# One projection for query, key and value of an attention unit, scored two steps after it

## The chip, the cores and the metric

The kernel runs on one core of one Trainium2 chip. The metric is the device time of one execution in microseconds (us). The core has five engines that run side by side, each through its own instructions in the order in which they are written: TensorE (PE in the profile; its weight loads are PEld), VectorE (DVE), ScalarE (ACT), GpSimd (POOL) and SyncE (SP, which here only starts DMA transfers). They wait for one another through semaphores.

## The reference

A trunk of two layers on 1024 tokens of width 1024: dilated attention, MLP, mLSTM, MLP, all with residuals. The change is in the attention, of which this is what is computed:

```
qkv = (x @ w_in).reshape(b, s, 3, 3 groups, 16 heads, 64)
for g, (window, dilation) in enumerate(((128, 1), (512, 4), (2048, 16))):
    q = rms_norm(qkv[:, :, 0, g], q_gain[g]) * 64 ** -0.5
    k = rms_norm(qkv[:, :, 1, g], k_gain[g])
    # causal; a query at t sees t, t-d, ..., t-window (129 keys at most)
    o, l = dilated_window_attention(q, k, qkv[:, :, 2, g], rel_bias[:, g], window, dilation)
wts = softmax over the three groups of the log-denominators l
y = sum over groups of wts * o;  x = x + y @ w_out
```

## The kernel before

The attention phase goes through 24 **sections**, one for each pair of heads (8) and group (3): section 3p+g is pair p, group g. A section has eight **tiles** of 128 tokens and eight **units** of 128 queries. All matmuls are "split": each f32 operand is held as a high part (`_hi`) and a rest (`_lo`), and `split_matmul` (L67) issues three matmuls, hi·hi (L69), lo·hi (L70), hi·lo (L71).

The work is written as **supersteps** `st` of eight **steps** `j` (`run_supersteps`; 4 supersteps in line, a loop of 3 rounds of 6, the rest in line). Every engine has its own `step(i, st, j)`, and the order in it is the order on that engine. A step `T = 8·st + j` of TensorE does, one after another:

- query and key of tile T (`ps_qk`): 8 row blocks k, three matmuls each with 256 columns; the stationary operand is the tile of the normed input, `hT_hi[:, k, j*P:(j+1)*P]`;
- three transposes into `ps_t`: normalised query and key of tile T-1 (`qkn`) and value (`vT`) of a tile of the section before; once in a while the row statistics `stat`;
- the transposes of the probabilities `prob` of unit U-1 into `ps_p`, where U = T-8: units are scored one superstep after their projection;
- a quarter of the value projection of half a section (`ps_v`), six matmuls of 512 columns, value transposed (`w_hi` stationary);
- the scores of unit U (`ps_s`), and probabilities times value of unit U-1 (`ps_o`, called the PV product below).

ScalarE in a step: exp of unit U-1 (`prob`, L635), copies of `ps_o` (L651, L652), the high part of a weight block (`w_hi`, L602), then `sq`, the squares of `ps_qk` of tile T (L667), which wait until that projection is done, then `pT_hi` (L673, the high part of the transposed probabilities), `qk_hi` (L684) and `v_hi` (L688). VectorE: bias and maximum of the unit's scores (L723, L726), `ss` and `var` (L732, L737) out of `sq`, `pT_lo` (L743), `qk_lo` (L758), `v_lo` (L764), `qkn` (L779), and in some steps the merge of the three groups of a pair (`merge_step`, L794 to L847). GpSimd: `w_lo` and the inverse root `rs`. SyncE loads the weight blocks 12 steps ahead.

Units of group 0 but for the first, and every second unit of group 1, also have the 128 keys before them (`has_prev`): their scores are 256 columns wide and their PV product has six matmuls instead of three. There are 88 of these **wide** units and 104 **narrow** ones. The tokens of groups 1 and 2 are reordered (stride 4, stride 16) when ScalarE and VectorE write `qk_hi`, `qk_lo` and `vT` (`perm_view`, `perm_dest`).

Of the kernel before, what the change touches and what calls it, by code (L numbers as in the profile page):

```python
# [29 lines left out]
NG = len(GROUPS)  # L30
HEADS = 16
# [17 lines left out]
def bias_onehot():  # L49

    out = np.zeros((NG, REL_BUCKETS + 1, BIAS_LEN), np.float32)
    exact = REL_BUCKETS // 2
    for g, (window, dilation) in enumerate(GROUPS):
        band = window // dilation
        for x in range(BIAS_LEN):
            step = x - (P - 1)
            if step < 0 or step > band:
# [16 lines left out]
def perm_view(ap, g, width):  # L74

    if g == 0:
        return ap
    return ap.rearrange("p (i r) -> p r i", r=GROUPS[g][1])


def perm_dest(buf, g, t0, width):

    if g == 0:
        return buf[:, t0:t0 + width]
    d = GROUPS[g][1]
    if g == 1:
        n, i0 = t0 // HALF, (t0 % HALF) // d
        return buf.rearrange("p (r n i) -> p r n i", r=d, n=2)[:, :, n, i0:i0 + width // d]  # L90
    return buf.rearrange("p (r i) -> p r i", r=d)[:, :, t0 // d:(t0 + width) // d]


def natural_view(buf, g):
# [5 lines left out]
    return buf.rearrange("p (r i) -> p i r", r=16)  # L100


def split_tokens(ap, g):
# [5 lines left out]
    return ap.rearrange("p (i r) -> p i r", r=16)  # L109


# [192 lines left out]
LAST_SUPER = SECTIONS + 2  # L304
# [18 lines left out]
class AttentionBuffers:  # L323


    def __init__(self, nc, ctx):
        sb = lambda n, s: ctx.enter_context(nc.sbuf_tensor(n, s, F32))
        self.vT = sb("vT", [P, 2, SEQ])
# [4 lines left out]
        self.x_tiles = [b[:, i, :] for b in (self.vT, self.o_g0, self.w_bc) for i in range(2)]  # L333
# [3 lines left out]
def attention_phase(nc, ones, ident, buffers, total, norm_gain, hT_hi, hT_lo, wqkv, q_gain, k_gain, bias_dram, yT_dram):  # L337
# [3 lines left out]
    with ExitStack() as ctx:  # L341
# [8 lines left out]
        qk_hi = sb("qk_hi", [P, 2, 2, SEQ], F32R)  # L350
        qk_lo = sb("qk_lo", [P, 2, 2, SEQ], F32R)
        v_hi = sb("v_hi", [P, 3, P], F32R)
        v_lo = sb("v_lo", [P, 3, P], F32R)
# [13 lines left out]
        vT, w_bc, prob = buffers.vT, buffers.w_bc, buffers.prob  # L367
        o_raw = [buffers.o_g0, total[:].rearrange("p (o t) -> p o t", o=1), buffers.o_g2]
        ring = sb("ring", [P, HALF])
        compact = sb("compact", [64, NG, 2, 2, 16])  # L370
        top = sb("top", [64, 2, 16])
        diff = sb("diff", [64, NG, 2, 16])
        grown = sb("grown", [64, NG, 2, 16])
        part = sb("part", [64, NG, 2, 16])
        den = sb("den", [64, 2, 16])
        share = sb("share", [64, NG, 2, 16])

        ps_qk = [ps(f"ps_qk{i}", [P, HALF]) for i in range(2)]
        ps_v = ps("ps_v", [P, HALF])
# [12 lines left out]
        qk_mm, v_mm, turned = sem("qk_mm"), sem("v_mm"), sem("turned")  # L392
# [4 lines left out]
        vT_done = sem("vT_done")  # L397
# [12 lines left out]
        def has_unit(st, j, back):  # L410

            return TT <= TT * st + j - back < TT * (SECTIONS + 1)

        def unit(st, j, back):

            sec, u = divmod(TT * (st - 1) + j - back, TT)
            return sec, u
# [6 lines left out]
        def _(sp):  # L424
# [4 lines left out]
            sp.dma_start(gains[HD:P, 1, :], k_gain).then_inc(gains_in, 16)  # L429
            for n in range(TT + 4):  # L430
# [4 lines left out]
            def step(i, st, j):  # L435
# [5 lines left out]
                if j == 2 and st < SECTIONS:  # L441
                    g, pair = st % NG, st // NG + 2 * i
                    if st >= NG:
                        sp.wait_ge(neg_done, TT * N - 2 * TT)
                    if st == 1:
                        norm.wait_all(sp)
                    base = (g * HEADS + 2 * pair) * BIAS_LEN
                    if g < 2:
                        sp.dma_start(bias[g][:], bass.AP(bias_dram.tensor, base, [[1, P], [BIAS_LEN, 2], [1, 2 * P]]))\
                            .then_inc(bias_in[g], 16)  # L450
                    else:
                        sp.dma_start(bias[g][0:64], bass.AP(bias_dram.tensor, base, [[1, 64], [BIAS_LEN, 2], [1, P]]))\
                            .then_inc(bias_in[g], 16)
                        sp.dma_start(bias[g][64:P, :, 0:64],
                                     bass.AP(bias_dram.tensor, base + 64, [[1, 64], [BIAS_LEN, 2], [1, 64]]))\
                            .then_inc(bias_in[g], 16)
                if j == 2 and 2 <= st <= SECTIONS + 1 and (st - 2) % NG < 2:
                    g, pair = (st - 2) % NG, (st - 2) // NG + 2 * i
# [5 lines left out]
                    for s in range(2):  # L464
                        for h in range(2):
                            src = stat_dram[g, s, h]
                            if g == 0:
                                sp.dma_start(compact[:, g, s, h, :], src.rearrange("(p c) -> p c", c=16))\
                                    .then_inc(compact_in[g], 16)
                            else:  # L470
                                sp.dma_start(compact[:, g, s, h, :].rearrange("p (r c) -> p r c", r=4),
                                             src.rearrange("(r p c) -> p r c", r=4, c=4)).then_inc(compact_in[g], 16)
                if j == 5 and st >= 4 and (st - 4) % NG == 0:
                    pair = (st - 4) // NG + 2 * i
                    sp.wait_ge(share_done, pair + 1)
                    sp.dma_start(share_dram.rearrange("g h (p c) -> p (g h) c", c=16),
# [6 lines left out]
                if j == 0 and st >= 5 and (st - 5) % NG == 0:  # L483
                    pair = (st - 5) // NG + 2 * i
# [1419 lines left out]
```

## Time and profile before

| | us |
|---|---|
| median of three runs | 3387.8 (3387.46 to 3390.41) |
| the profiled execution | 3383.74 |
| its span, first to last instruction | 3382.0 |
| TensorE busy over the span | 3192.3 (94%) |
| VectorE, ScalarE, GpSimd busy | 1334.0, 1102.1, 825.2 |
| mean granted TensorE clock | 0.978 of full |

The attention phase reaches from the first `ps_qk` matmul at 34.94 us to the first matmul of the next phase at 1332.47 us. The last projection matmul of it starts at 1266.80 us; what follows until 1332.47 is the tail: the last section's units, the last merge, the store of its result and the load of it by the next phase. Starts of instructions in a timeline are exact to 0.01 us; a matmul's duration is longer than the distance to the next one, since matmuls overlap in the array, so that distances between starts are what they cost. In the same way an instruction of ScalarE or VectorE may be started before the one ahead of it has ended.

### The profile page before, as it was taken

Reading aid. Unit: us, or ns where it says so; the run is one execution under the profiler, and the core shown is the slowest. Engines: PE = TensorE matmul, PEld = TensorE weight load, DVE = VectorE, ACT = ScalarE, POOL = GpSimd, SP = SyncE. Lnnn points to the kernel's source line nnn. Section 1 sums busy time; section 2 is a strip of 40 time slices with the busy share of each in tenths; the row PEclk is TensorE's granted clock in tenths of the full one; section 3 lists DMA queues with packets and bytes.
Section 4 is the critical chain, followed back from the end, with each engine's and each line's share of the span. In section 5 each row is a group of like instructions: output and inputs, shape, how many; then the busy total and the mean of one; then the engine's idle time right before and its main releaser. Section 6 shows DMA issues by size and latency. Waiting matters only on the chain. (4 is left out here: it accounts for less than half of the span.)

```text
span 3382.0 us, 48256 instructions
## 1 busy us (share of the span) xinstructions
PE 3192.3 (94%) x17466; PEld 2669.5 (79%) x17466; DVE 1334.0 (39%) x3725; ACT 1102.1 (33%) x3002; POOL 825.2 (24%) x598
## 2 busy tenths in 40 slices
PE   4999999999999995999999999899877999999999
PEld 3888888888888883878888888678655788888887
DVE  6445454555555554341313133541064431313131
ACT  4555555555555553321111112210244211111020
POOL 3332333333233320212222122112111122222221
PEclk9999999999999995999999999999998999999999
DMA  2112121211112114111111111111201111111112
GB/s 98 36 40 59 41 58 40 61 49 50 52 45 53 47 32 150 50 44 47 48 50 44 50 50 45 38 44 50 81 26 57 44 50 44 50 50 44 50 45 80
DMA packets 89904, 177.01 MB, mean 52 GB/s; under 512 B 25515, under 2 KB 55870, under 8 KB 89662
## 3 DMA queue, kind: packets, MB, share of 16 engines
q1 hardware_dynamic: 87358, 169.63, 16.1%
q10 hardware_dynamic: 2304, 4.20, 0.3%
q8 instruction: 147, 2.41, 0.3%
q14 instruction: 95, 0.78, 0.1%
HBM read 160.67 MB, written 13.12 MB: 51 GB/s over the span
## 5 line engine op out<-in xcount | busy, mean ns | idle before, releaser
L69 PE MATMUL ps_qk<-w_hi,attn_hT_hi 128*128 128x256 f32 x1536 | 437.4, 285 | 23.3 <-DVE attn_hT_lo L213 9.7
L915 POOL TENSOR_TENSOR first_w_lo<-first_raw,first_w_hi 128x1024 fp32r<-128x1024 f32 x96 | 231.7, 2414 | 900.8 <-ACT first_w_hi L911 900.8
L70 PE MATMUL ps_qk<-w_lo,attn_hT_hi 128*128 128x256 f32 x1536 | 436.1, 284 | 0.0
L71 PE MATMUL ps_qk<-w_hi,attn_hT_lo 128*128 128x256 f32 x1536 | 436.1, 284 | 0.0
L857 POOL TENSOR_TENSOR w_lo<-raw,w_hi 128x384 fp32r<-128x384 f32 x192 | 194.6, 1015 | 701.9 <-ACT w_hi L602 701.9
L915 POOL TENSOR_TENSOR second_w_lo<-second_raw,second_w_hi 128x1024 fp32r<-128x1024 f32 x72 | 172.2, 2391 | 630.0 <-ACT second_w_hi L911 630.0
L69 PEld LDWEIGHTS ps_qk<-w_hi,attn_hT_hi 128*128 128x128 f32 x1536 | 294.1, 191 | 27.6 <-issue 13.3
L635 ACT ACTIVATE prob<-ps_s,neg_max 128x128 f32<-128x128 f32 (+1 forms) x384 | 156.6, 413 | 439.7 <-DVE neg_max L726 439.7
L70 PEld LDWEIGHTS ps_qk<-w_lo,attn_hT_hi 128*128 128x128 f32 x1536 | 294.7, 192 | 0.4
L71 PEld LDWEIGHTS ps_qk<-w_hi,attn_hT_lo 128*128 128x128 f32 x1536 | 294.9, 192 | 0.0
L69 PE MATMUL first_ps<-first_hid_hi,first_w_hi 128*128 128x512 f32 x640 | 255.4, 399 | 32.7 <-DVE first_hid_lo L1239 32.7
L732 DVE TENSOR_REDUCE ss<-sq 128x4 f32<-128x256 f32 x192 | 80.7, 420 | 506.9 <-ACT sq L667 506.9
L69 PE MATMUL first_ps<-first_hT_hi,first_w_hi 128*128 128x512 f32 x640 | 252.6, 395 | 14.2 <-POOL first_w_lo L915 14.2
L69 PE MATMUL second_ps<-second_hid_hi,second_w_hi 128*128 128x512 f32 x640 | 251.0, 392 | 12.5 <-DVE second_hid_lo L1242 12.5
L70 PE MATMUL first_ps<-first_hid_lo,first_w_hi 128*128 128x512 f32 x640 | 254.9, 398 | 0.0
L71 PE MATMUL first_ps<-first_hid_hi,first_w_lo 128*128 128x512 f32 x640 | 254.7, 398 | 0.0
L70 PE MATMUL first_ps<-first_hT_lo,first_w_hi 128*128 128x512 f32 x640 | 251.4, 393 | 0.0
L71 PE MATMUL first_ps<-first_hT_hi,first_w_lo 128*128 128x512 f32 x640 | 251.4, 393 | 0.0
L70 PE MATMUL second_ps<-second_hid_lo,second_w_hi 128*128 128x512 f32 x640 | 250.5, 391 | 0.0
L71 PE MATMUL second_ps<-second_hid_hi,second_w_lo 128*128 128x512 f32 x640 | 250.1, 391 | 0.0
L879 POOL TENSOR_TENSOR rs<-var,minus_half 128x4 f32<-128x4 f32 x192 | 193.3, 1007 | 133.5 <-DVE var L737 125.0
L911 ACT CAST first_w_hi<-first_raw 128x1024 fp32r<-128x1024 f32 x96 | 99.9, 1041 | 383.6 <-PE first_ps L71 358.5
(276 smaller groups left out, 6853.9 us busy)
## 6 DMA issues: line engine op xcount, KB each, us to landing
raw<-in_wqkv SPq DMA_DIRECT2D x192, 192.0 KB, 2.3
first_raw<-in_w SPq DMA_DIRECT2D x64, 512.0 KB, 3.4
second_raw<-in_w SPq DMA_DIRECT2D x64, 512.0 KB, 3.4
w_bc<-share_dram SPq DMA_DIRECT2D x48, 256.0 KB, 4.2
first_raw<-in_vo_pieces SPq DMA_DIRECT2D x16, 512.0 KB, 3.5
bias<-bias_dram SPq DMA_DIRECT2D x16, 256.0 KB, 3.6
yT_dram<-o_g SPq DMA_DIRECT2D x8, 512.0 KB, 3.1
first_raw<-in_attn_wo SPq DMA_DIRECT2D x8, 512.0 KB, 3.5
```

Of the source, the lines that this page charges most:

```text
L69: pe.matmul(out, a_hi, b_hi, start=first, stop=False)
L70: pe.matmul(out, a_hi, b_lo, start=False, stop=False)
L71: return pe.matmul(out, a_lo, b_hi, start=False, stop=last)
L635: a = act.activation(prob[:, u % 2, h, c0:2 * P], ps_s[h][:, c0:2 * P], ACT.Exp, bias=neg_max[:, sp_, h * TT + u:h * TT + u + 1], accum_ou ...
L732: dve.tensor_reduce(ss[:], sq[:].rearrange("p (h e) -> p h e", e=HD), AX.X, ALU.add)\
L857: pool.tensor_tensor(w_lo[:, par, k, :], raw[:, slot, :], w_hi[:, par, k, :].bitcast(F32), ALU.subtract).then_inc(w_lo_done, 1)
L879: pool.tensor_tensor(rs[:], var[:], minus_half[:], ALU.pow).then_inc(rs_done, 1)
L911: act.copy(self.hi[:, n % 2, :], self.raw[:, n % self.RAW, :]).then_inc(self.hi_done, 1)
L915: pool.tensor_tensor(self.lo[:, n % 2, :], self.raw[:, n % self.RAW, :], self.hi[:, n % 2, :].bitcast(F32), ALU.subtract).then_inc(self.lo ...
```

## The change

A section's value is projected together with its query and key: each tile has one projection of 384 columns into `ps_qkv`, 24 matmuls. The value comes out with its tokens on the partitions, so that `vT`, its copies and its transposes go; ScalarE writes `v_hi` and VectorE `v_lo` straight from `ps_qkv`. The reordering of tokens moves to the stationary operand: the tile of group 1 reads the normed input with a stride of 4 elements, that of group 2 with a stride of 8 (`tile_view`), where a unit of group 2 now mixes two residues and the bias masks the other one. With that a tile is a unit, and units are scored two steps after their projection (`LAG = 2`) instead of eight. The projection is cut in two: five of its eight row blocks, then the transposes of `qkn` and `prob`, then the last three blocks. `qk_hi`, `qk_lo` hold one section instead of two. The merge has one copy less and stands at other steps; the tail has one superstep less. In the diff `LAG` is 2 and `EARLY_TILES` is 5; the wait on `v_lo_done` stands ahead of the PV product, beside those on `pT_hi` and `pT_lo`; `turned_probabilities` writes `pT_hi`.

```
-            U = T - TT
+            U = T - LAG
@@ TensorE
-                for k in range(KT):
-                    mm = split_matmul(pe, ps_qk[j % 2][:, 0:2 * P],
-                                      hT_hi[:, k, j * P:(j + 1) * P], hT_lo[:, k, j * P:(j + 1) * P],
-                                      w_hi[:, par, k, 0:2 * P], w_lo[:, par, k, 0:2 * P], k == 0, k == KT - 1)
-                mm.then_inc(qk_mm, 1)
+            def project(k_first, k_end):
+                for k in range(k_first, k_end):
...
+                    mm = split_matmul(pe, ps_qkv[j % 2][:, 0:W3],
+                                      tile_view(hT_hi[:, k, :], st % NG, j), tile_view(hT_lo[:, k, :], st % NG, j),
+                                      w_hi[:, par, k, :], w_lo[:, par, k, :], k == 0, k == KT - 1)
+                return mm
+            if st < SECTIONS:
...
+                project(0, EARLY_TILES)
...
-                    mm = pe.transpose(ps_t[:, 2 * P:3 * P], vT[:, (st - 1) % 2, j * P:(j + 1) * P], ident[:])
...
-                for k in range(2 * (j % 4), 2 * (j % 4) + 2):
-                    mm = split_matmul(pe, ps_v[:], w_hi[:, par, k, 2 * P:3 * P], w_lo[:, par, k, 2 * P:3 * P],
-                                      hT_hi[:, k, half * HALF:(half + 1) * HALF],
-                                      hT_lo[:, k, half * HALF:(half + 1) * HALF], k == 0, k == KT - 1)
+                project(EARLY_TILES, KT).then_inc(qkv_mm, 1)
...
+                pe.wait_ge(v_lo_done, U)
@@ ScalarE
-                act.copy(perm_dest(vT[:, vp, :], g, HALF, HALF), perm_view(ps_v[:], g, HALF)).then_inc(vT_done, 1)
...
-                act.wait_ge(qk_mm, T + 1)
+                act.wait_ge(qkv_mm, T + 1)
                 if TT * st + j >= 1:
                     act.wait_ge(reduced, T)
-                act.activation(sq[:], ps_qk[j % 2][:, 0:2 * P], ACT.Square).then_inc(squared, 1)
+                act.activation(sq[:], ps_qkv[j % 2][:, 0:2 * P], ACT.Square).then_inc(squared, 1)
+                act.copy(v_hi[:, j, :], ps_qkv[j % 2][:, 2 * P:W3]).then_inc(v_hi_done, 1)
...
+            turned_probabilities()
@@ VectorE
+                dve.wait_ge(v_hi_done, T + 1)
...
+                dve.tensor_tensor(v_lo[:, j, :], ps_qkv[j % 2][:, 2 * P:W3], v_hi[:, j, :].bitcast(F32), ALU.subtract)\
+                    .then_inc(v_lo_done, 1)
@@ reordering
+def tile_view(ap, g, u):
+    if g == 0:
+        return ap[:, u * P:(u + 1) * P]
     if g == 1:
+        return ap.rearrange("p (n i r) -> p r n i", n=2, r=4)[:, u // 2, u % 2, :]
+    return ap.rearrange("p (m u) -> p u m", u=TT)[:, u, :]
```

What now stands where. First TensorE, from the end of one tile's projection on; in it `ps_qk` and `ps_qkv` are the projections, `ps_s` the scores, `ps_o` the PV product, rows that only repeat are left out. Before:

```order
L71 MATMUL ps_qk<-w_hi,attn_hT_lo 128x256
L526 MATMUL ps_t<-ident,qkn 128x128 x2
L530 MATMUL ps_t<-ident,vT 128x128
L547 MATMUL ps_p<-ident,prob 128x128 x2
L69 MATMUL ps_v<-attn_hT_hi,w_hi 128x512
...
L71 MATMUL ps_s<-qk_hi,qk_lo 128x128
L69 MATMUL ps_o<-pT_hi,v_hi 128x256
```

And now:

```order
L75 MATMUL ps_qkv<-w_hi,attn_hT_lo 128x384
L517 MATMUL ps_t<-ident,qkn 128x128 x2
L534 MATMUL ps_p<-ident,prob 128x128 x4
L73 MATMUL ps_qkv<-w_hi,attn_hT_hi 128x384
...
L75 MATMUL ps_qkv<-w_hi,attn_hT_lo 128x384
L73 MATMUL ps_s<-qk_hi 128x256
...
L75 MATMUL ps_s<-qk_hi,qk_lo 128x256
L73 MATMUL ps_o<-pT_hi,v_hi 128x256
```

Between the last matmul of a tile's projection and the PV product there stood the transposes, a quarter of the value projection and the scores; now only the scores stand there.

Then ScalarE, in the middle of a step: `sq` is the instruction that waits for the tile's projection, `pT_hi` what the PV product waits for. Before:

```order
L602 CAST w_hi<-raw 128x384
L664 REGISTER_ALU
L667 ACTIVATE sq<-ps_qk 128x256
L673 CAST pT_hi<-ps_p 128x512
L684 ACTIVATE qk_hi<-ps_t,gains 128x4x32 x2
L688 CAST v_hi<-ps_t 128x128
```

And now:

```order
L577 CAST w_hi<-raw 128x384
L630 REGISTER_ALU
L633 ACTIVATE sq<-ps_qkv 128x256
L634 CAST v_hi<-ps_qkv 128x128
L640 CAST pT_hi<-ps_p 128x512
L648 ACTIVATE qk_hi<-ps_t,gains 128x128 x2
```

`v_hi` has moved from behind `pT_hi` to ahead of it; `pT_hi` stands behind `sq` in both.

## Rows read from the trace of the kernel before

**Rows 1.** Busy time by stretch: inside the attention, and its tail.
```profile
core 0: us, PE busy (x) PEld busy (x) DVE busy (x) ACT busy (x) POOL busy (x), PEclk, DMA share, GB/s
400.00:500.00 100.00, 96.54 (x722) 85.59 (x721) 58.09 (x223) 53.23 (x185) 30.31 (x30) 1.00 0.20 56
1269.00:1333.00 64.00, 24.47 (x107) 17.10 (x108) 23.41 (x91) 19.58 (x79) 2.34 (x1) 0.52 0.26 79
```

**Rows 2.** Timeline of TensorE, one wide step: start, us, operation.
```profile
1033.96 0.38 PE L526 MATMUL ps_t<-ident,qkn 128*128 128x128 f32 x2
1034.17 0.27 PE L530 MATMUL ps_t<-ident,vT 128*128 128x128 f32 x1
1034.28 0.60 PE L547 MATMUL ps_p<-ident,prob 128*128 128x128 f32 x4
...
1034.95 0.39 PE L70 MATMUL ps_v<-attn_hT_lo,w_hi 128*128 128x512 f32 x1
...
1035.88 0.40 PE L71 MATMUL ps_v<-attn_hT_hi,w_lo 128*128 128x512 f32 x1
1036.20 0.39 PE L69 MATMUL ps_s<-qk_hi 64*128 64x256 f32 x2
...
1036.77 0.38 PE L69 MATMUL ps_o<-pT_hi,v_hi 128*128 128x256 f32 x1
...
1037.57 0.28 PE L69 MATMUL ps_qk<-w_hi,attn_hT_hi 128*128 128x256 f32 x1
...
1040.32 0.29 PE L71 MATMUL ps_qk<-w_hi,attn_hT_lo 128*128 128x256 f32 x1
1040.44 0.38 PE L526 MATMUL ps_t<-ident,qkn 128*128 128x128 f32 x2
```

**Rows 3.** Timeline of ScalarE, the same step and the next.
```profile
1034.85 0.39 ACT L667 ACTIVATE sq<-ps_qk 128x256 f32<-128x256 f32 x1
1035.13 0.58 ACT L673 CAST pT_hi<-ps_p 128x512 fp32r<-128x512 f32 x1
...
1036.11 0.28 ACT L688 CAST v_hi<-ps_t 128x128 fp32r<-128x128 f32 x1
1036.31 0.59 ACT L625 COPY vT<-ps_v 128x512 f32<-128x512 f32 x1
...
1039.44 0.20 ACT L635 ACTIVATION_READ_ACCUMULATOR prob<-ps_s,neg_max 128x1 f32 x1
...
1040.64 0.38 ACT L667 ACTIVATE sq<-ps_qk 128x256 f32<-128x256 f32 x1
```

**Rows 4.** Timeline of VectorE, the same step.
```profile
1035.26 0.42 DVE L732 TENSOR_REDUCE ss<-sq 128x4 f32<-128x256 f32 x1 [2.62 <-ACT sq L667]
1035.72 0.23 DVE L737 TENSOR_SCALAR var<-ss 128x4 f32<-128x4 f32 x1
1035.86 0.68 DVE L743 TENSOR_TENSOR pT_lo<-ps_p,pT_hi 128x512 fp32r<-128x512 f32 x1
```

**Rows 5.** Groups by form, 0 to 1400 us: narrow units.
```profile
L743 DVE TENSOR_TENSOR pT_lo<-ps_p,pT_hi 128x256 fp32r<-128x256 f32 x104 | 44.0, 423 | 16.5 <-ACT pT_hi L673 16.2
...
L673 ACT CAST pT_hi<-ps_p 128x256 fp32r<-128x256 f32 x104 | 38.9, 374 | 17.0 <-PE ps_p L547 17.0
```

**Rows 6.** Timeline of GpSimd in the first section, where no units run.
```profile
84.82 1.01 POOL L879 TENSOR_TENSOR rs<-var,minus_half 128x4 f32<-128x4 f32 x1 [2.49 <-DVE var L737]
...
89.29 1.01 POOL L879 TENSOR_TENSOR rs<-var,minus_half 128x4 f32<-128x4 f32 x1 [2.48 <-DVE var L737]
```

**Rows 7.** Timelines of TensorE and VectorE in the tail.
```profile
1266.80 0.40 PE L71 MATMUL ps_v<-attn_hT_hi,w_lo 128*128 128x512 f32 x1
...
1300.05 0.42 DVE L743 TENSOR_TENSOR pT_lo<-ps_p,pT_hi 128x256 fp32r<-128x256 f32 x1 [2.03 <-ACT pT_hi L673]
...
1300.58 0.55 PE L69 MATMUL ps_o<-pT_hi,v_hi 128*128 128x256 f32 x1 [0.97 <-DVE pT_lo L743]
```

**Rows 8.** Groups by form: merge operations, with strided and with contiguous reads.
```profile
L837 DVE TENSOR_TENSOR w_bc<-w_bc,total 128x1024 f32<-128x1024 f32 x8 | 16.0, 2003 | 0.9 <-DMA w_bc<-share_dram 0.9
...
L840 DVE TENSOR_TENSOR o_g<-o_g,w_bc 128x1024 f32<-128x1024 f32 x8 | 9.7, 1213 | 0.0
```

More of the change, by code:

```diff
@@ L54, in bias_onehot @@
         band = window // dilation
+        mixed = dilation // UNIT_STRIDE[g]
         for x in range(BIAS_LEN):
-            step = x - (P - 1)
-            if step < 0 or step > band:
+            step, other = divmod(x - (P - 1), mixed)
+            if step < 0 or step > band or other:
                 out[g, REL_BUCKETS, x] = 1.0
@@ L349, in attention_phase @@
         gains = sb("gains", [P, 2, NG])
[L350 to L353, printed above, removed]
+        qk_hi = sb("qk_hi", [P, 2, SEQ], F32R)
+        qk_lo = sb("qk_lo", [P, 2, SEQ], F32R)
+        v_hi = sb("v_hi", [P, TT, P], F32R)
+        v_lo = sb("v_lo", [P, TT, P], F32R)
         sq = sb("sq", [P, 2 * P])
@@ L366, in attention_phase @@
         stat_rows = sb("stat_rows", [4 * TT, P])
-        vT, w_bc, prob = buffers.vT, buffers.w_bc, buffers.prob
+        w_bc, prob = buffers.w_bc, buffers.prob
         o_raw = [buffers.o_g0, total[:].rearrange("p (o t) -> p o t", o=1), buffers.o_g2]
         ring = sb("ring", [P, HALF])
[L370 to L379, printed above, removed]
+        compact = sb("compact", [P, NG, 2, 2, TT])
+        top = sb("top", [P, 2, TT])
+        diff = sb("diff", [P, NG, 2, TT])
+        grown = sb("grown", [P, NG, 2, TT])
+        part = sb("part", [P, NG, 2, TT])
+        den = sb("den", [P, 2, TT])
+        share = sb("share", [P, NG, 2, TT])
+        ps_qkv = [ps(f"ps_qkv{i}", [P, HALF]) for i in range(2)]
         ps_t = ps("ps_t", [P, HALF])
@@ L429, in _, with load_bias @@
             sp.dma_start(gains[HD:P, 1, :], k_gain).then_inc(gains_in, 16)
+            def load_bias(g, pair):
+                base = (g * HEADS + 2 * pair) * BIAS_LEN
+                width = 2 * P if g < 2 else P
+                sp.dma_start(bias[g][:], bass.AP(bias_dram.tensor, base, [[1, P], [BIAS_LEN, 2], [1, width]]))\
+                    .then_inc(bias_in[g], 16)
+            load_bias(0, 0)
             for n in range(TT + 4):
@@ L440, in step @@
                     sp.dma_start(raw[:, j % 4], wqkv[T + 12]).then_inc(raw_in[j % 4], 16)
[L441 to L445, printed above, removed]
-                        norm.wait_all(sp)
[L447 to L458, printed above, removed]
+                if j == 5 and st + 1 < SECTIONS:
+                    if st + 1 >= NG:
+                        sp.wait_ge(neg_done, TT * N - TT)
+                    if st == 0:
+                        norm.wait_all(sp)
+                    load_bias((st + 1) % NG, (st + 1) // NG + 2 * i)
+                if j == 4 and 1 <= st <= SECTIONS and (st - 1) % NG < 2:
+                    g, pair = (st - 1) % NG, (st - 1) // NG + 2 * i
                     rows = 2 * pair + g + 1
@@ L768, in step @@
-                if j == 0:
-                    turned_tiles()
-                    turned_probabilities()
-                else:
-                    turned_probabilities()
-                    turned_tiles()
+                turned_probabilities()
+                if 1 <= TT * st + j <= TT * SECTIONS:
+                    dve.wait_ge(turn_hi, T)
+                    if j == 3 and st >= 1 and (st - 1) % NG < 2:
+                        if st >= 2:
+                            dve.wait_ge(rows_out, 16 * (2 * ((st - 1) // NG + 2 * i) + (st - 1) % NG))
+                        dve.tensor_copy(stat_rows[:], ps_t[0:4 * TT, 3 * P:4 * P]).then_inc(rows_done, 1)
+                    sec, t = divmod(TT * st + j - 1, TT)
+                    g = sec % NG
+                    for a in range(2):
+                        ins = dve.scalar_tensor_tensor(qk_lo[:, a, t * P:(t + 1) * P], ps_t[:, a * P:(a + 1) * P],
+                                                       gains[:, a, g:g + 1], qk_hi[:, a, t * P:(t + 1) * P].bitcast(F32),
+                                                       ALU.mult, ALU.subtract)
+                    ins.then_inc(turn_lo, 1)
```

218 lines of the change are left out of this document (76 added, 142 removed).

## The prediction, made before the changed kernel had run

> **What bounds the kernel now.** I first read busy time by stretch: inside the attention TensorE is busy 96.5 of 100 us at a granted clock of 1.00, the others 30 to 58 us [rows 1]. So TensorE sets the pace there, and a change to the attention is worth what it does to TensorE's step. The tail is different: 24.5 us busy in 64, clock 0.52 (the 1.2 GHz level) [rows 1]; there a chain through all engines sets the pace.
>
> Then I read one wide step on TensorE, start to start: it takes 40.44 - 33.96 = 6.48 us. Its 24 projection matmuls of 256 columns take 40.44 - 37.57 = 2.87 us, 0.120 each; a value matmul of 512 columns takes (35.88 - 34.95)/4 = 0.233; the transpose of vT 0.11; scores 0.57, PV 0.80 [rows 2]. The reader is to see that there is no hole: what PV needs is ready when TensorE comes to it. Last, the same step on ScalarE and VectorE [rows 3, 4], for what is ready when. It shows how far the feeding chain is from its limit: pT_lo ends at 1035.86 + 0.68 = 1036.54 and PV starts at 1036.77, 0.23 us later. That cover was the transposes, the value matmuls and the scores, which stand between a tile's projection and PV.
>
> **The change, part by part.**
>
> *TensorE's own work.* vT's transpose goes, -0.11 per step. 24 matmuls of 256 and 6 of 512 columns (24 x 0.120 + 6 x 0.233 = 4.27) become 24 of 384. No row has 384 columns; between 0.120 and 0.233 that is 0.176, sum 4.23, so -0.03 with the last digits kept. Together -0.14 us per step, if the stationary operand read with a stride costs nothing (below).
>
> *The wait that is new.* In a step of the changed program TensorE goes: five blocks, transposes (prob of unit U-1 among them), three blocks, scores, PV of unit U-1. ScalarE makes pT_hi for that PV behind sq, and sq waits for the whole projection, whose end now lies behind the transposes. So pT_hi cannot start while the last three blocks run, though its input is there, and v_hi is put ahead of it as well. Let 0 be the start of the last projection matmul. Its result is out at about 0.34 (0.29 at 256 columns, 0.40 at 512 [rows 2]). sq followed a projection's end by 0.03 (40.32 + 0.29 to 40.64 [rows 2, 3]): sq at 0.37. The next on ScalarE, v_hi, 0.28 later (34.85 to 35.13), pT_hi 0.20 behind v_hi (36.11 to 36.31) [rows 3]: pT_hi at 0.85. It takes 0.58 (wide) [rows 3] or 0.37 (narrow) [rows 5], so it ends at 1.43 or 1.22. VectorE meanwhile: ss at 0.37 + 0.39 + 0.02 = 0.78, var 0.46 and pT_lo at the earliest another 0.14 later, 1.38 [rows 4]. So pT_lo starts at 1.46 (wide, after pT_hi, with 0.03 for the hop) or 1.38 (narrow, after var); it takes 0.68 [rows 4] or 0.42 [rows 5] and ends at 2.14 or 1.80. TensorE began PV 0.11 after pT_lo's end where it had waited for it (1300.05 + 0.42 to 1300.58 [rows 7]): PV at 2.25 or 1.91. Without a wait TensorE would be there at 0.27 + 0.57 = 0.84: the last matmul 0.18 plus the 0.09 by which 35.88 to 36.20 exceeds 0.233, then the scores [rows 2]. The wait is 1.41 us in wide and 1.07 us in narrow steps.
>
> Behind the waiting PV on TensorE is the whole next projection, and for its end sq of the next step waits: nothing catches up, each step pays. There are 88 wide units and 104 narrow ones [rows 5], of which the last three run behind the last projection. 88 x (1.41 - 0.14) = 112 and 101 x (1.07 - 0.14) = 94, together **+206 us**.
>
> *The other ring: exp.* The transposes of prob wait for exp, which waits for the maxima, which stand on VectorE behind pT_lo, qk_lo and qkn. Before, exp of the next unit ended at 39.64, 4.79 us after sq's start at 34.85 [rows 3]. Now v_hi ahead of pT_hi adds 0.20 to ScalarE's part of it and the late v_lo changes nothing, so exp ends near 0.37 + 4.79 + 0.20 = 5.36. TensorE comes to those transposes at 2.25 + 0.80 (PV) + 15 x 0.176 + 0.21 (qkn) = 5.90 in a wide step. It is hidden, by 0.5 us; had PV not waited it would be the bound, at 4.49 against 5.36. The merge on VectorE (up to 2.00 us in one step [rows 8]) uses that slack up and pushes some steps. It did before too: the exp that ended at 39.64 ran 1.1 us ahead of the transposes that followed 0.33 us after 40.44 [rows 2, 3]. The slack has shrunk by half a microsecond in the seven or so merging steps of a pair, while a copy has gone: 0 to +25 us over 8 pairs. I take 0, since the merge is the same work and several of its pieces are shorter than the slack, and keep the 25 in the range.
>
> *Starting early and the tail.* Six steps of the first section now carry units. Without units a step took 89.29 - 84.82 = 4.47 us [rows 6], with a wide one 6.48: six times 2.0 less the first narrow unit's part is **+11 us**. In the tail 1300.58 - 1266.80 = 33.8 us go by from the last projection matmul to the last PV [rows 7], ten steps of 3.4 us. Now three steps are left, of which the first also ends a loaded one: 3 x 3.4 + 2.5 = 12.7, **-21 us**. The merge, store and load behind it are the same in length. SyncE's queue has the same transfers per step, one bias transfer less per pair, and the weight blocks are loaded 12 steps ahead as before, now with longer steps.
>
> *Sum.* +206 + 11 - 21 = **+196 us**. The profiled execution took 3383.7 us (span 3382.0 and 1.7 around it) and the median of the runs is 3387.8, 4.1 more; 3387.8 + 196 = **3584 us**.
>
> *What I can't read here: the strided weight load.* 128 of the 192 tiles (groups 1 and 2) load their stationary operand with a stride of 4 or 8 elements; no row shows TensorE doing that. From below: a transpose loads new weights too and takes 0.11 us (34.17 to 34.28 [rows 2]), so the load can be that long at most; VectorE's reads with a stride took 2003 / 1213 = 1.65 times as long [rows 8]; 0.11 x 1.65 = 0.18, against 0.176 for the matmul that hides it: +0.005 x 24 x 128 = 15 us. From above: if it took twice as long, 0.22, then 0.044 x 24 x 128 = +135 us, all of it on the path, since the projection lies in the ring. Less than nothing it can't cost. I take 0, nearest to the 1.65. The Trainium skill (SBUF — State Buffer, section "Door 1: The DMA port swizzle") speaks against this change: it says that SBUF is read in lines of 16 bytes, and that an access which moves to a new line each time pays for it; strides of 4 and 8 f32 do that at every element. It gives no figure for the penalty, so what it makes of the time is a number between the two ends just named. Rows 8 agree in kind, on another engine.
>
> **Rivals.**
> (a) *The strided load is slower than the matmul*, on top of the wait: for it rows 8, against it that 0.07 us of room is there (0.176 less 0.11). It gives 3584 + 15 to 135, about 3660 in the middle; the sections of groups 1 and 2 would be slow and those of group 0 not. This is also what the rule on lines above would do.
> (b) *PV does not wait*: faster. If pT_hi and pT_lo came in the time of the scores, TensorE would keep its pace: 189 x 0.14 = 26, and 10 from start and tail, 3388 - 36 = 3352. The exp ring (5.36 against 4.49) would have to be shorter than its rows too. It decides at a mean wait of 0.14 + 10/189 = 0.19 us per step; pT_lo would have to end before 0.92 after the last projection matmul, where sq alone ends at 0.76. Everything in the order speaks against it.
> (c) *The clock falls*, since TensorE now idles over a microsecond in every step. In the tail it is at 1.2 GHz where it works 38% of the time; but at 400 to 500 us, where merges make holes too, it stayed at 1.00 [rows 1], and TensorE will still be at work about 80% of the time. At half the clock 24 matmuls cost 0.15 more each: 3.5 us per step, far above 4000 us.
>
> **How the numbers follow.** The forecast has 0.63; its own range is 3535 to 3640, since 0.25 us per step in the chain of four hops is 47 us. (a) has 0.25, (b) 0.07, (c) 0.03, a wait much shorter than computed 0.02. The range for 8 in 10 leaves out (b), (c) and the upper end of (a): 3510 to 3720. The measurement can tell about 0.2%, 7 us, from no change. Faster 0.07, within 0.2% 0.01, slower 0.92.
>
> **What would show it.** In the profile after: TensorE idle ahead of the ps_o matmuls, released by pT_lo on VectorE, about 1.4 and 1.1 us, 189 times, some 230 us in all; TensorE's busy share in the attention down to about 80%; wide steps near 7.75 and narrow ones near 6.8 us; distances between ps_qkv matmuls of 0.176 us in all three groups; last PV some 13 us after the last projection. Wrong it would be if TensorE waited in front of the transposes of prob (the exp ring) or not at all, or if the spacing differed between groups.

## The result, and the profile after

The changed kernel takes 3802.0 us (median of 4 runs), the kernel before 3387.6 us: a ratio of 1.122, 95% interval 1.1201 to 1.124. That is +414 us where +196 were forecast. The direction and its mechanism came as predicted; the size lies outside the range.

First the busy time by stretch after, in the columns of [rows 1] (TensorE, its weight loads, VectorE, ScalarE, GpSimd, clock, DMA): a section of group 0, one of group 1, and the whole attention.

```profile
core 0: us, PE busy (x) PEld busy (x) DVE busy (x) ACT busy (x) POOL busy (x), PEclk, DMA share, GB/s
900.00:950.00 50.00, 41.67 (x256) 38.38 (x255) 22.16 (x98) 22.28 (x80) 12.10 (x12) 1.00 0.21 51
1000.00:1050.00 50.00, 43.89 (x211) 41.97 (x212) 16.49 (x66) 16.77 (x62) 11.06 (x11) 0.90 0.11 35
...
63.33:1702.20 1638.87, 1391.37 (x7482) 1312.57 (x7483) 646.04 (x2620) 616.24 (x2270) 376.50 (x374) 0.97 0.13 35
```

TensorE was busy 96.5 of 100 us; now it is 41.7 of 50. In group 1 there are 211 matmuls in the 50 us against 256 in group 0, and yet TensorE is busy longer: each matmul has become slower there, and the clock stands at 0.90. Two things went wrong, then: TensorE waits, and two groups of three run slower.

The wait is the one forecast. Timeline of TensorE, a wide step of group 0, where [rows 2] had no hole:

```profile
926.34 0.34 PE L75 MATMUL ps_qkv<-w_hi,attn_hT_lo 128*128 128x384 f32 x1
...
926.95 0.28 PE L75 MATMUL ps_s<-qk_hi,qk_lo 64*128 64x256 f32 x2
928.57 0.36 PE L73 MATMUL ps_o<-pT_hi,v_hi 128*128 128x256 f32 x1 [1.34 <-ACT pT_hi L640]
```

ScalarE and VectorE in that step, beside [rows 3, 4]:

```profile
926.72 0.39 ACT L633 ACTIVATE sq<-ps_qkv 128x256 f32<-128x256 f32 x1 [1.92 <-PE ps_qkv L75]
927.00 0.26 ACT L634 CAST v_hi<-ps_qkv 128x128 fp32r<-128x128 f32 x1
927.15 0.60 ACT L640 CAST pT_hi<-ps_p 128x512 fp32r<-128x512 f32 x1
```
```profile
927.13 0.42 DVE L684 TENSOR_REDUCE ss<-sq 128x4 f32<-128x256 f32 x1 [4.34 <-ACT sq L633]
927.59 0.17 DVE L689 TENSOR_SCALAR var<-ss 128x4 f32<-128x4 f32 x1
927.78 0.69 DVE L695 TENSOR_TENSOR pT_lo<-ps_p,pT_hi 128x512 fp32r<-128x512 f32 x1
```

Counted from the start of the last projection matmul (926.34), sq came at 0.38, pT_hi at 0.81, pT_lo at 1.44 and PV at 2.23; the prediction had 0.37, 0.85, 1.46 and 2.25. (In the narrow step whose last projection matmul starts at 1702.21, PV came at 1.90 where 1.91 was forecast.) Note how the wait is labelled: "pT_hi" on ScalarE, though pT_lo on VectorE ends last (928.47, against 927.75). Where the engine named had long been done, look for the one that ended just before the waiter began.

The group's row in the page says what it comes to over the kernel; the list of waits, before and after, has the second ring (columns: in total, times, longest):

```profile
L73 PE MATMUL ps_o<-pT_hi,v_hi 128*128 128x256 f32 x280 | 95.8, 342 | 221.7 <-ACT pT_hi L640 220.4
```
```profile
PE ps_p L547 <- ACT prob L635: 19.8, 22, 1.4
```
```profile
PE ps_o L73 <- ACT pT_hi L640: 220.4, 189, 1.4
...
PE ps_p L534 <- ACT prob L602: 21.9, 25, 1.3
```

TensorE waited 220 us for PV, 189 times, where 88 x 1.41 + 101 x 1.07 = 232 were forecast. For exp (the ps_p row) it waited about as long as before in total.

What had not been counted shows in group 1: the same projection, matmul start to matmul start.

```profile
1001.37 0.39 PE L73 MATMUL ps_qkv<-w_hi,attn_hT_hi 128*128 128x384 f32 x1
1001.60 0.39 PE L74 MATMUL ps_qkv<-w_lo,attn_hT_hi 128*128 128x384 f32 x1
1001.83 0.39 PE L75 MATMUL ps_qkv<-w_hi,attn_hT_lo 128*128 128x384 f32 x1
...
1006.65 0.52 PE L73 MATMUL ps_qkv<-w_hi,attn_hT_hi 128*128 128x384 f32 x1
1006.97 0.52 PE L74 MATMUL ps_qkv<-w_lo,attn_hT_hi 128*128 128x384 f32 x1
```

The spacing is 0.233 us. In group 2 it is 0.24:

```profile
1701.73 0.40 PE L73 MATMUL ps_qkv<-w_hi,attn_hT_hi 128*128 128x384 f32 x1
1701.97 0.40 PE L74 MATMUL ps_qkv<-w_lo,attn_hT_hi 128*128 128x384 f32 x1
```

In group 0 it is 0.17 (0.174 over the fourteen from 929.36 to 931.79):

```profile
923.76 0.33 PE L73 MATMUL ps_qkv<-w_hi,attn_hT_hi 128*128 128x384 f32 x1
923.93 0.33 PE L74 MATMUL ps_qkv<-w_lo,attn_hT_hi 128*128 128x384 f32 x1
```

The weight load in front of each lasts 0.33 us instead of 0.19; one of group 0, then one of group 1:

```profile
923.93 0.19 PEld L75 LDWEIGHTS ps_qkv<-w_hi,attn_hT_lo 128*128 128x128 f32 x1
...
1001.41 0.33 PEld L74 LDWEIGHTS ps_qkv<-w_lo,attn_hT_hi 128*128 128x128 f32 x1
```

From 1006.65 to 1006.97 the spacing is 0.32: here the granted clock stands at 0.50 of full, the 1.2 GHz level, for about three microseconds:

```profile
1006.00:1008.00 2.00, 2.00 (x8) 2.00 (x8) 0.89 (x7) 1.03 (x6) 0.00 (x0) 0.50 0.02 4
```

There are three such falls between 1000 and 1050, and so this stretch shows 0.90. Last the end of the attention: the last projection matmul starts at 1702.21 and the last PV at 1715.90, 13.7 us later (12.7 forecast, 33.8 before [rows 7]).

### The profile page after: what moved, and what is told of

Read it like the earlier page. It is cut to its first block and busy times, and to the rows that moved or that the text cites. A ratio compares the mean times of both kernels' runs of the same rounds, so it can differ in the third digit from the quotient of the medians.

```text
span 3800.2 us, 45658 instructions
## 1 busy us (share of the span) xinstructions
PE 3393.2 (89%) x16122; PEld 2924.4 (77%) x16122; DVE 1332.0 (35%) x3716; ACT 1063.5 (28%) x2954; POOL 825.2 (22%) x598
## 5 line engine op out<-in xcount | busy, mean ns | idle before, releaser
L73 PE MATMUL ps_qkv<-w_hi,attn_hT_hi 128*128 128x384 f32 x1536 | 628.4, 409 | 23.8 <-DVE attn_hT_lo L204 10.3
L74 PE MATMUL ps_qkv<-w_lo,attn_hT_hi 128*128 128x384 f32 x1536 | 595.6, 388 | 0.0
L75 PE MATMUL ps_qkv<-w_hi,attn_hT_lo 128*128 128x384 f32 x1536 | 593.9, 387 | 0.0
L73 PEld LDWEIGHTS ps_qkv<-w_hi,attn_hT_hi 128*128 128x128 f32 x1536 | 434.8, 283 | 28.6 <-issue 13.8
L74 PEld LDWEIGHTS ps_qkv<-w_lo,attn_hT_hi 128*128 128x128 f32 x1536 | 441.1, 287 | 0.0
L75 PEld LDWEIGHTS ps_qkv<-w_hi,attn_hT_lo 128*128 128x128 f32 x1536 | 440.4, 287 | 0.0
L73 PE MATMUL ps_o<-pT_hi,v_hi 128*128 128x256 f32 x280 | 95.8, 342 | 221.7 <-ACT pT_hi L640 220.4
```

The source lines that it names most:

```text
L73: pe.matmul(out, a_hi, b_hi, start=first, stop=False)
L74: pe.matmul(out, a_hi, b_lo, start=False, stop=False)
L75: return pe.matmul(out, a_lo, b_hi, start=False, stop=last)
```

## The experiments

Two theories for what the forecast lacked. **L**: a weight load with this stride takes a time of its own that is longer than the matmul beside it (the first expectations call this theory S). **H**: the difference comes from TensorE's holes (longer waits, a lower clock; there it is rival W). And inside the forecast: does PV wait because of the order on ScalarE and VectorE, and is exp's ring really 0.5 us behind it?

**Contiguous tiles in the changed kernel.** Group 0's view for all:

```diff
-    if g == 0:
-        return ap[:, u * P:(u + 1) * P]
-    if g == 1:
-        return ap.rearrange("p (n i r) -> p r n i", n=2, r=4)[:, u // 2, u % 2, :]
-    return ap.rearrange("p (m u) -> p u m", u=TT)[:, u, :]
+    return ap[:, u * P:(u + 1) * P]
```

> The changed kernel with tile_view returning the contiguous tile for all three groups (leaves out the reordering of the tokens of groups 1 and 2, so its output is not the reference's; all else, the order of all engines too, stays). Theory S (the strided weight load is the larger part of what the forecast missed): the ps_qkv matmuls of all groups stand 0.174 us apart as those of group 0 do in the changed kernel (0.233 in groups 1 and 2), 24 x 0.06 x 128 = 184 us go, the clock dips shorten things by little: about 3610 us, near the forecast of 3584. PV still waits, about 1.2 us x 189. Rival W (the wait and the clock dips are the larger part): under 60 us go, 3740 us or more.

Measured 3604.8 us (1.0669 of before, 1.0626 to 1.0712). The ps_qkv matmuls now stand 0.17 to 0.18 us apart in all three groups. So 197 us of the 414 hang on the stride and 217 on the rest, 196 of them forecast. The holes are the same in both kernels, so H is out as the main cause. The waits of TensorE in this run:

```profile
PE ps_o L73 <- ACT pT_hi L636: 219.5, 189, 1.4
PE ps_p L530 <- ACT prob L598: 39.2, 37, 2.0
```

PV waits as it did. TensorE waits 39.2 us for exp, 19.4 more than before. By the timelines 34.1 us of them (28 waits) stand behind merge pieces on VectorE, against 14.3 us (14 waits) before: that is the merges' term, which the prediction took at 0 in a range of 0 to 25. Over this attention the granted clock was 0.98:

```profile
63.33:1504.00 1440.67, 1177.89 (x7479) 1079.78 (x7480) 646.06 (x2620) 616.19 (x2270) 377.18 (x374) 0.98 0.15 40
```

**A stride in the kernel before.** The other way round: only the stationary operand of ps_qk is changed, to the strided view.

```diff
-  hT_hi[:, k, j * P:(j + 1) * P], hT_lo[:, k, j * P:(j + 1) * P],
+  tile_view(hT_hi[:, k, :], st % NG, j), tile_view(hT_lo[:, k, :], st % NG, j),
```

> The kernel before with one edit: the stationary tile of the query and key projection is read with stride 4 in group 1 and 8 in group 2 (its tokens then come in the wrong order, so the output is not the reference's). No wait of the change is in it. Theory L (a strided load has a rate of its own, 0.233 us for 128 columns, and a matmul shorter than that is bound by it): the 256-column matmuls go from 0.120 to 0.233 apart in 128 of 192 tiles, 24 x 0.113 x 128 = 348 us, about 3720. Rival A (a strided load adds a fixed 0.06 us to each matmul, whatever its length): 184 us, about 3570.

Measured 3715.1 us (1.0966, 1.0948 to 1.0984). Its projection, in matmuls of 256 columns that were 0.120 apart [rows 2]:

```profile
599.66 0.40 PE L69 MATMUL ps_qk<-w_hi,attn_hT_hi 128*128 128x256 f32 x1
599.90 0.40 PE L70 MATMUL ps_qk<-w_lo,attn_hT_hi 128*128 128x256 f32 x1
```

They are 0.24 apart (a section of group 2; 0.23 to 0.24 in group 1). No wait of the new order exists in this kernel and the matmul is shorter, and yet the distance is the same as with 384 columns. The load sets it: theory L. (0.12 x 3072 loads is 369 us against 328 measured; 14 of the missing 41 are the waits for exp behind merges, since of the 19.8 us of waits for exp before only the 5.5 of the tail are left here. The rest wasn't taken apart.)

**Strides of 2 and 3.** In the changed kernel the view of group 1 gets a stride of 2 elements, group 2's a stride of 3.

```diff
-        return ap.rearrange("p (n i r) -> p r n i", n=2, r=4)[:, u // 2, u % 2, :]
-    return ap.rearrange("p (m u) -> p u m", u=TT)[:, u, :]
+        return ap.rearrange("p (n i r) -> p r n i", n=4, r=2)[:, u % 2, u // 2, :]
+    return ap[:, 80 * u:80 * u + 3 * P - 2:3]
```

> The changed kernel with the stationary tile of group 1 read with a stride of 2 elements and that of group 2 with a stride of 3 (wrong tokens in them, so the output is not the reference's); group 0 contiguous. Read is the distance between ps_qkv matmuls in the sections of each group. Theory of lines (a load pays where no two of its elements share 16 bytes): stride 2 has two elements in every line and stays at 0.174 us; stride 3 has two in one line of three and lies in between or near 0.174; only strides of 4 and more are at 0.233. Rival (any stride but 1 has the same slow rate): 0.233 in both groups and 3800 us.

One run, 3613.4 us, against 3604.8 with contiguous tiles. Group 1 (stride 2), then group 2 (stride 3):

```profile
180.09 0.34 PE L73 MATMUL ps_qkv<-w_hi,attn_hT_hi 128*128 128x384 f32 x1
180.26 0.34 PE L74 MATMUL ps_qkv<-w_lo,attn_hT_hi 128*128 128x384 f32 x1
...
222.61 0.35 PE L75 MATMUL ps_qkv<-w_hi,attn_hT_lo 128*128 128x384 f32 x1
222.79 0.35 PE L73 MATMUL ps_qkv<-w_hi,attn_hT_hi 128*128 128x384 f32 x1
```

0.175 to 0.18: behind a 384-column matmul strides of 2 and 3 elements cost next to nothing, strides of 4 (16 bytes) and 8 cost alike. The loads themselves are longer already at 2 and at 3 elements, 0.25 us against 0.19:

```profile
180.09 0.25 PEld L74 LDWEIGHTS ps_qkv<-w_lo,attn_hT_hi 128*128 128x128 f32 x1
...
222.80 0.25 PEld L74 LDWEIGHTS ps_qkv<-w_lo,attn_hT_hi 128*128 128x128 f32 x1
```

The matmul of 384 columns hides that. Whether one of 256 columns (0.120) would, no run shows.

**Probabilities first.** pT_hi is put ahead of sq and v_hi on ScalarE, pT_lo ahead of ss and var on VectorE; once with the strided tiles, once with contiguous ones.

```diff
+                turned_probabilities()
                 if st < SECTIONS:
                     act.wait_ge(qkv_mm, T + 1)
...
                     act.copy(v_hi[:, j, :], ps_qkv[j % 2][:, 2 * P:W3]).then_inc(v_hi_done, 1)
-                turned_probabilities()
```

> The changed kernel with one move: pT_hi stands ahead of sq on ScalarE (ahead of its wait for the whole projection), and pT_lo ahead of ss on VectorE. Strided tiles stay. Theory S with the ring through sq and pT as forecast: TensorE's idle time ahead of ps_o (222 us) goes to under 20, the exp ring stays hidden since the strided projection is 1.4 us longer than its rows in group 0; the clock dips go with the holes (20 us): 3802 - 216 - 20 = about 3565 us. Rival (another wait takes its place, the transposes of prob waiting for exp): less than half of it comes back, 3680 or more.

> Both edits together (leaves out the reordering of tokens, as the first). Theory S: what is left is TensorE's own work, 0.14 us per step less than before, and 10 us from start and tail: about 3355 us, plus what the exp ring adds in merging steps, up to 25: 3355 to 3380, a little faster than the kernel before. Rival (the exp ring binds once PV does not wait, 0.4 us or more per step): 3430 or more.

Measured 3650.7 (1.0783, 1.0765 to 1.0801) and 3548.3 us (1.0474, 1.0457 to 1.0492). The waits for PV are gone from the list; of the 220 us only 151 and 57 came back. The lists of waits, of the strided and of the contiguous one:

```profile
PE ps_p L534 <- ACT prob L602: 96.3, 93, 2.0
```
```profile
PE ps_p L530 <- ACT prob L598: 178.9, 173, 2.9
```

The exp ring has taken the place of PV, in nearly every step of the contiguous kernel (173 waits) and in half of those of the strided one (93). Both expectations had this as the rival only, and their times were too low by 86 and by some 170 us. The prediction had put it 0.5 us behind the PV wait and said that it would bind if PV did not wait. With strided tiles the longer projection hides some of it, which is also why the two kernels differ by only 102 us and not by 197.

**Maxima first.** In the two kernels with the probabilities first: on VectorE the maxima of a unit stood in the step after its scores, behind qkn, v_lo and the merge piece. Moved into the step of the scores, ahead of qkn (contiguous tiles, then strided ones):

```diff
-                if has_unit(st, j, 1):
-                    sec, u = unit(st, j, 1)
...
+                if has_unit(st, j, 0):
+                    sec, u = unit(st, j, 0)
...
+                    dve.wait_ge(scored, U + 1)
```

> The third experiment (contiguous tiles, probabilities first) with one more move: on VectorE the bias and maxima of the unit just scored stand ahead of qkn, in the time in which VectorE waits for rs of GpSimd, instead of behind qkn and v_lo. It leaves out the reordering of tokens. Theory (the exp ring binds there: 168 us idle ahead of ps_p): exp comes 1.2 us earlier, no ring is longer than TensorE's own work, and that is 0.14 us a step less than before: 3352 to 3380 us, the clock dips gone too. Rival (qkn, now about 1 us later, becomes the wait ahead of ps_t, or ps_p still waits): 3430 or more.

> The second experiment (strided tiles as in the changed kernel, probabilities first) with maxima first as well; it computes the reference. Theory: TensorE's own work alone is left, 3352 plus 128 x 24 x 0.06 = 184 for the strided loads: 3536 to 3560 us. Rival (a wait other than that for exp): over 3610.

Measured 3327.6 us (0.9826, 0.981 to 0.9842) and 3519.9 us (1.0394, 1.0377 to 1.0412). With contiguous tiles:

```profile
60.00:1233.00 1173.00, 1151.74 (x7485) 1069.61 (x7485) 660.38 (x2623) 637.12 (x2275) 381.54 (x376) 0.99 0.18 49
```

and with strided ones:

```profile
60.00:1400.00 1340.00, 1328.59 (x7372) 1264.98 (x7372) 653.14 (x2584) 629.84 (x2242) 377.47 (x373) 0.99 0.16 43
```

In both TensorE is busy 98 and 99% of the attention at a clock of 0.99. This pair prices the stride nearly free of waits: 3519.9 - 3327.6 = 192.3 us, 0.0626 us for each of 24 x 128 loads. And without the stride the new structure is 60 us faster than the kernel before (a bound, not a kernel to use: it reads the wrong tokens): merging the projections was sound, its two side effects were not. Both times lie some 20 us below what was expected; the expectations had left in the waits for exp behind merges that the kernel before has (14.3 us), and these went too.

**Staging the tiles.** If the stride costs only in the weight load, another engine can make contiguous copies two steps ahead. (To make room for them, small tensors such as sq and compact share memory with the first input tiles.) First both parts, the high one by ScalarE and the low one by GpSimd:

```diff
+  stage_tile(st, j, 0, hT_hi, lambda out, src: act.copy(out, src).then_inc(staged_hi, 1))
...
+  stage_tile(st, j, 1, hT_lo, lambda out, src: pool.tensor_copy(out, src).then_inc(staged_lo, 1))
```

> The same orders as the last one, and the tiles of groups 1 and 2 are copied into contiguous buffers two steps ahead (high part by ScalarE behind qk_hi, rest by GpSimd behind rs), so that TensorE loads nothing with a stride; it computes the reference. Small tensors share memory with the first input tiles to make room. Theory (ScalarE has 6.0 - 4.1 us idle in a step and its copy of 1024 elements takes 1.0 to 1.7, GpSimd has 4 us and takes 2.4 to 4): distances of 0.174 in all groups, 3360 to 3400 us. Rival (one of the copies delays exp or rs, since ScalarE and GpSimd stand in the rings): 3430 or more, with waits ahead of ps_p or ps_t in the sections of groups 1 and 2.

Measured 3492.5 us (1.0311, 1.0294 to 1.0328): the loads are fast again (0.19 us), but only 27 us are won, where 120 to 160 were expected. TensorE waits for qkn on VectorE instead (13.1 us, 3 times, in the strided kernel without the copies), by the list of waits:

```profile
PE ps_t L538 <- DVE qkn L741: 117.8, 129, 10.8
```

The row of neg_max (durations: minimum, median, maximum in ns) and two instructions of the timeline show why:

```profile
L733 DVE TENSOR_SCALAR neg_max<-stat x192: 168/1612/2106, 75.0 to 1407.6; 128x2 f32<-128x2 f32 x192
```
```profile
708.53 2.18 POOL L840 CAST st_lo<-attn_hT_lo 128x1024 fp32r<-128x1024 f32 x1
...
708.72 2.02 DVE L733 TENSOR_SCALAR neg_max<-stat 128x2 f32<-128x2 f32 x1
```

neg_max has two elements per row. It takes 0.17 us, but 2.02 here: it ends with GpSimd's copy (710.74 and 710.71). The timeline has the same in every case: 128 of the 192 neg_max start while a copy runs on GpSimd, and they take 1.29 to 2.11 us; the other 64 take 0.17. To see whether GpSimd or ScalarE does that, the high part alone is staged; the low part stays strided, and the small tensors stay where they were:

```diff
-  stage_tile(st, j, 1, hT_lo, lambda out, src: pool.tensor_copy(out, src).then_inc(staged_lo, 1))
...
-  left = [staged[j % 2][a][:, k, :] for a in range(2)]
+  left = [staged[j % 2][0][:, k, :], tile_view(hT_lo[:, k, :], st % NG, j)]
```

> The kernel with the probabilities and the maxima first (3519.9 us), whose tiles of h are strided; here ScalarE copies the high part of each tile of groups 1 and 2 to a contiguous one two steps ahead (2.18 us of its time), and only the low part, 8 of the 24 loads of such a step, is read with a stride. Theory L (each strided load costs 0.06 us that nothing hides): 16 x 0.06 x 128 = 123 us go, 3397 us; spacing 0.175 for the 16 and 0.233 for the 8. In the run where GpSimd copied the low part as well VectorE's neg_max rose from 0.17 to 2 us and the time was 3492.5. Theory G (GpSimd's copy, running beside it, holds up VectorE): neg_max is back at 0.17 us here, and the time lies below 3440 us. Rival S (it is ScalarE's copy in the step that delays exp, and neg_max only waits for what that delays): neg_max stays long or TensorE waits for prob as much as there, and the time stays at 3460 us or above.

Measured 3388.8 us (1.0005, 0.9996 to 1.0015), and neg_max is back:

```profile
L732 DVE TENSOR_SCALAR neg_max<-stat x192: 169/170/174, 75.0 to 1300.9; 128x2 f32<-128x2 f32 x192
```

```profile
905.41 0.34 PE L74 MATMUL ps_qkv<-w_lo,st_hi 128*128 128x384 f32 x1
905.59 0.40 PE L75 MATMUL ps_qkv<-w_hi,attn_hT_lo 128*128 128x384 f32 x1
905.83 0.34 PE L73 MATMUL ps_qkv<-w_hi,st_hi 128*128 128x384 f32 x1
```

Theory G holds. (It isn't the small tensors' new place either: in the next experiment they have moved too, and neg_max takes 0.17 us.) From the matmul with the strided load to the next it is 0.24 us (905.59 to 905.83), between its contiguous neighbours 0.17 to 0.18: the price is one per load and adds up, 3519.9 - 3388.8 = 131 us for 16 loads in 24 and 3388.8 - 3327.6 = 61 us for the other 8.

**The low part too, between the merges.** VectorE copies it at the end of its step, but not in steps with a large merge piece; TensorE reads those tiles with the stride.

```diff
+  if not merging(st, j):
+      stage_tile(st, j, 1, hT_lo, lambda out, src: dve.tensor_copy(out, src).then_inc(staged_lo, 1))
```

> As the kernel with the high part of the tiles staged by ScalarE (3388.8 us), and now VectorE copies the low part too, at the end of its step, in the 88 of the 128 cases in which that step has no large merge piece; in the other 40 TensorE still reads the low part with a stride. Theory L: 8 x 0.06 x 88 = 42 us go, 3347 us, under the 3360.2 us of the kernel before with its maxima moved. VectorE is idle 3.6 us in a wide step without a merge piece and the copy takes about 2.1 us. Rival: the copy stands ahead of pT_lo and ss of the next step, which delays rs and exp: TensorE waits for prob or for pT_lo in those steps and the time is 3370 us or above. Rival: two engines that read h with a stride at once slow each other (ScalarE's copy above 2.6 us instead of 2.1): 3388 us or more.

Measured 3355.5 us (0.9911, 0.9898 to 0.9925), 33 us below the kernel that stages the high part alone, where 42 were expected. (It was 93 tiles and not 88, since the first pair has no merge before it: by the theory 45.) Rows of the two copies:

```profile
L684 ACT CAST st_hi<-attn_hT_hi x128: 2027/2148/2316, 97.8 to 1249.1; 128x1024 fp32r<-128x1024 f32 x128
...
L761 DVE CAST st_lo<-attn_hT_lo x93: 1067/1123/1265, 100.0 to 1251.0; 128x1024 fp32r<-128x1024 f32 x93
```

ScalarE's copy takes as long as without VectorE's (2.15 us), so the two don't visibly slow each other. Of the missing 12 us 4 are waits for exp (6.0 us against 1.9 with the high part alone); the rest wasn't taken apart.

**The same repair in the kernel before.** There too a merge piece stands ahead of the maxima. They are moved into the step of the scores, once ahead of qkn (the same edit as above), once behind it and ahead of the merge.

> The kernel before with one thing moved: VectorE takes the maxima of the unit just scored at the end of the same step, in front of qkn and the merge, instead of at the start of the next. Theory R (a merge piece stands ahead of the maxima and so delays exp and the transposes of prob; about 4.7 us of such waits per pair are seen before): 20 to 35 us go, 3355 to 3367 us. Rival: VectorE now waits for the scores in every step, qkn is late and TensorE waits for qkn instead: 3390 us or more, with waits of PE on DVE qkn in the list of waits. Rival: the waits at merges come from another engine, no change within 0.2%.

> As the kernel before with the maxima taken in the step of the scores, but behind qkn and in front of the merge piece. Theory R: the same 20 to 35 us go, since the merge piece is behind the maxima here too, and qkn isn't held up: 3350 to 3367 us. Rival: exp comes later by qkn's 0.4 us and a part of the waits stays: 3370 to 3388 us.

Measured 3360.2 and 3360.3 us, both 0.9922 (0.9909 to 0.9936) of before. Of the 19.8 us of waits for exp 4.4 and 5.6 are left, eight waits each, those of the tail: the ones behind merges are gone. That is theory R, though the time fell by 27 us and the waits by 15 alone; qkn is not held up. Against this repaired kernel the best form of the change (3355.5) has no lead that the intervals can tell: the gain of the merged projection is there (3360.2 - 3327.6 = 33 us), but strided tiles or their copies cost most of it.

## Why the prediction was wrong

**The step that failed** is the term "stationary operand read with a stride", taken as 0 out of 0 to 135 us. The working was: a load takes 0.11 us at most, VectorE's strided reads took 1.65 times as long, so 0.18 against the 0.176 of the matmul beside it. Measured, such a load allows one matmul in 0.233 to 0.24 us, with 256 columns as with 384, and costs 192 us. That the spacing would differ between the groups is what the prediction itself had named as a sign of being wrong. The cost is above even the upper bound, which had doubled 0.11 to 0.22. The 1.65 was a ratio of another engine, for an operation that reads and writes with a stride, and VectorE's plain copy of these very tiles shows none of it (1.12 us for 1024 elements, against 1.21 for the contiguous tensor_tensor of [rows 8]). A ratio from one engine is no price for another, not even as the nearest row. And the trace before had rows of the loads themselves, which the prediction didn't read:

```profile
L71 PEld LDWEIGHTS ps_qk<-w_hi,attn_hT_lo 128*128 128x128 f32 x1536 | 294.9, 192 | 0.0
```

0.19 us, not 0.11, beside matmuls 0.120 apart. The record of such a load is 0.07 us longer than the distance it allowed; so 0.19 x 1.65 - 0.07 = 0.24 would have been an estimate for the strided one, some 200 us. With a ratio of VectorE in it, that it meets the measurement may be luck; but it would have shown that 0 was not the nearest value.

The rule of the Trainium skill that was weighed then (SBUF — State Buffer, section "Door 1: The DMA port swizzle": lines of 16 bytes, and a price for each access that moves to a new line) was right in sign. TensorE's step fits its line size: strides of 8 and 12 bytes cost next to nothing behind this matmul, 16 and 32 bytes cost alike. The loads fit it less well, since they last longer at 8 and 12 bytes already (0.25 us against 0.19, and 0.33 at 16 and 32). Rival (a) named this mechanism, at 0.25, and had the sections of groups 1 and 2 slow and those of group 0 not; that is what the profile shows. Its size was again too small.

**The PV wait** was right: 220 us over 189 steps against 232, each hop of the chain within 0.04 us. The contiguous run gives what hangs on all but the stride: 217 us against 196. **TensorE's own work** was right (0.174 instead of 0.176), the **tail** too (13.7 us against 12.7). The +11 us of the early start were not measured by themselves.

**The merges** were taken as 0 with 25 kept in the range. By the waits for exp behind merge pieces (14.3 us before) they cost 20 us with contiguous tiles (34.1) and 4 in the changed kernel (18.0). That the longer strided projection hides the rest is argued, not shown.

**The clock** was named as rival (c) in a form that was too coarse: all or nothing. It fell for short stretches instead. A mean of 0.97 over 1638.9 us says that about 6%, 98 us, ran at 1.2 GHz; there matmuls are 0.32 apart and not 0.233, so some 98 x (1 - 0.233/0.32) = 27 us are lost, an estimate, since the 0.97 is rounded (0.965 to 0.975 would be 22 to 31 us). What preceded a fall is a row of steps with a hole of about a microsecond each; without the holes (maxima first) the clock was 0.99, and in three others that kept holes of one kind or the other (contiguous tiles, and probabilities first with either tile) it was 0.98. So the falls go with the holes, but their cause was not isolated.

**The sum**, from its parts: 220.4 (PV) - 26 (own work) - 10 (start and tail) + 4 (merges) + 192 (stride) + 27 (clock) = 407 of 414 us. Not all of it is measured in this kernel: the 192 is a difference of two others, the 27 is an estimate, and the -36 is the forecast's own. It is borne out by the contiguous kernel with the maxima first and the kernel before with the same repair (3327.6 - 3360.2 = -33). The 7 left were not taken apart.

**The exp ring** stood where the prediction had put it: behind the PV wait and ready to take its place. It did so the moment PV's operands came in time, in both runs; the prediction had its price too, 5.36 - 4.49 = 0.87 us a step with contiguous tiles, where 178.9 / 173 = 1.03 us were measured, merges included.

## What to carry to other kernels

A stationary operand read at a stride of 16 bytes or more has a price of its own per load, 0.233 to 0.24 us for 128 columns here, so a matmul would need some 512 columns or more to hide it (an estimate: [rows 2] has 0.233 for 512 columns; no run tried it), or the tile must be laid out or copied first. When work moves from before a wait to behind it, follow each operand of the next matmul through the in-order queues of the other engines: the instruction it stands behind sets its time, and two rings within half a microsecond of each other have to be cured together. Before comparing a restructured kernel with the old one, give the old one the same small repair.

## What the runs showed of the hardware that had not been expected

- Weight loads of 128 columns: one lasts 0.19 us contiguous, 0.25 with a stride of 2 or 3 elements of 4 bytes, 0.33 with 4 or 8. Behind matmuls of 384 columns strides of 2 and 3 leave 0.175 to 0.18 us a matmul; 4 and 8 make it 0.233 to 0.24, behind 256 columns as behind 384.
- A copy on GpSimd (2.18 us) held a two-element VectorE operation for its whole length: 0.17 became 2.02 us, and so in all 128 cases in which the copy was running when it started. Without that copy neg_max never took over 174 ns; but in those kernels no GpSimd operation ran while it did, so they don't tell whether the shorter w_lo and rs (1.01 us) would hold it too. The Trainium skill (SBUF — State Buffer, section "Who interferes with whom") says that VectorE, in some of its modes, and GpSimd share a pair of ports, which the one that comes first holds for a whole instruction; the two rows that end together agree.
- VectorE copied a tile with a stride of 4 or 8 elements in 1.12 us, ScalarE in 2.15, GpSimd in 2.11 (medians).
- TensorE's clock fell to 1.2 GHz for about three microseconds at a time (1005.66 to 1008.89) in a stretch where it was busy 43.9 of 50 us.
